# Applying the second layer's input-norm weight to the projection's weight pieces instead of to the transposed rows

## The reference

```python
def rms_norm(x, w):
    xf = x.astype(jnp.float32)
    xf = xf * lax.rsqrt(jnp.mean(xf * xf, axis=-1, keepdims=True) + RMS_EPS)
    return (xf * w.astype(jnp.float32)).astype(x.dtype)
...
    for layer in range(DEPTH):
        j = layer // 2
        h = rms_norm(x, norm_mix_w[layer])
...
            mix = retention_mixer(h, odd_w_in[j], ret_norm_w[j], odd_w_out[j])
        x = x + mix
        h = rms_norm(x, norm_ffn_w[layer])
        x = x + hierarchical_moe(h, router_c_w[layer], router_c_b[layer], router_f_w[layer], router_f_b[layer],
                                 moe_w_gate_up[layer], moe_w_down[layer])
...
def retention_mixer(h, w_in, norm_w, w_out):
    q, k, v, g = split_cols(h @ w_in, ODD_SPLITS)
```

## Time and profile before

| | us |
|---|---|
| median of 3 runs | 1178.06 (1177.57 to 1178.78) |
| profiled execution | 1180.1 |
| its span | 1178.3 |
| PE busy (share of the span) | 1111.0 (94%) |
| DVE busy | 699.3 (59%) |
| ACT busy | 608.7 (52%) |
| POOL busy | 395.7 (34%) |
| chain that ended last: PE / DVE / DMA / ACT | 83% / 7% / 3% / 3% |

### The profile page before, as it was taken

How to read it: one execution, slowest core, us unless ns; L and a number is a source line. 1 busy time by engine, 2 the same in 40 slices (tenths; PEclk the granted TensorE clock), 3 DMA queues, 4 the chain that set the end, 5 groups by cost and what they waited for, 6 DMA issues and landing times.

```text
span 1178.3 us, 19724 instructions
## 1 busy us (share of the span) xinstructions
PE 1111.0 (94%) x7062; PEld 912.4 (77%) x7063; DVE 699.3 (59%) x1016; ACT 608.7 (52%) x903; POOL 395.7 (34%) x344
## 2 busy tenths in 40 slices
PE   8999999999998899998999999999999997999990
PEld 5778887778787688886788888888888886788870
DVE  5435444368736999996646341543432138999975
ACT  5556234242434699995633342233342234899971
POOL 4343221110133244332155325442234442344332
PEclk8999999999999899999999999999999998999995
DMA  9333311112225699996443213331222364999945
GB/s 263 77 88 55 73 38 55 36 41 70 72 64 210 244 358 379 382 365 225 181 128 98 81 56 106 94 108 58 81 73 90 98 198 161 355 381 377 381 191 223
DMA packets 81668, 194.76 MB, mean 165 GB/s; under 512 B 20349, under 2 KB 21433, under 8 KB 80825
## 3 DMA queue, kind: packets, MB, share of 16 engines
q1 hardware_dynamic: 59368, 159.34, 40.2%
q10 hardware_dynamic: 12432, 17.60, 4.4%
q0 software_dynamic: 9792, 16.80, 3.8%
HBM read 189.50 MB, written 23.07 MB: 180 GB/s over the span
## 4 chain that ended last, share of the span: by engine, by line
PE 83%; DVE 7%; DMA 3%; ACT 3%; issue 1%; ACTq 1%; POOL 0%; POOLq 0%; DVEq 0%
PE ps L673 24%; PE ps L675 23%; PE ps L674 23%; PE ps L2572 2%; PE ps L2364 2%; DMA arena<-y 1%; DVE x L1469 1%; PE ps L2247 1%; ACTq L1423 1%; PE ps L2500 1%; DMA arena<-hs,slot_rows 1%; PE ps L2637 1%; PE ps L2201 1%; ACT wh L1006 1%; DMA y<-arena,cur_rows 1%
## 5 line engine op out<-in xcount | busy, mean ns | idle before, releaser
L840 POOL TENSOR_TENSOR wl<-raw,wh 128x1024 fp32r<-128x1024 f32 x94 | 228.6, 2440 | 380.4 <-ACT wh L1006 380.1
L673 PE MATMUL ps<-wh,hT_hi 128*128 128x512 f32 x864 | 347.3, 402 | 2.9 <-DVE hT_lo L1988 2.4
L675 PE MATMUL ps<-wh,hT_lo 128*128 128x512 f32 x864 | 338.4, 392 | 0.0
L674 PE MATMUL ps<-wl,hT_hi 128*128 128x512 f32 x864 | 337.9, 391 | 0.0
L1006 ACT ACTIVATE wh<-raw 128x1024 fp32r<-128x1024 f32 x116 | 122.4, 1068 | 213.0 <-PE ps L675 191.3
L673 PEld LDWEIGHTS ps<-wh,hT_hi 128*128 128x128 f32 x864 | 163.1, 189 | 38.1 <-DVE hT_lo L1988 2.9
L675 PEld LDWEIGHTS ps<-wh,hT_lo 128*128 128x128 f32 x864 | 162.6, 188 | 34.5
L674 PEld LDWEIGHTS ps<-wl,hT_hi 128*128 128x128 f32 x864 | 163.0, 189 | 30.7
L673 PE MATMUL ps<-hT_hi,wh 128*128 128x512 f32 (+1 forms) x296 | 117.0, 395 | 2.0 <-DVE arena_rounded L1820 1.0
L1963 DVE TENSOR_TENSOR wl<-arena,wh 128x1024 fp32r<-128x1024 f32 x96 | 113.6, 1222 | 5.6 <-ACT wh L1293 5.3
L674 PE MATMUL ps<-hT_lo,wh 128*128 128x512 f32 (+1 forms) x296 | 114.5, 387 | 0.0
(11 more groups left out here) (331 smaller groups left out, 1581.1 us busy)
## 6 DMA issues: line engine op xcount, KB each, us to landing
raw<-in_moe_w_gate_up_dram SPq DMA_DIRECT2D x64, 512.0 KB, 9.7
arena<-in_moe_w_gate_up_dram SPq DMA_DIRECT2D x64, 512.0 KB, 9.6
raw<-in_odd_w_in_dram SPq DMA_DIRECT2D x48, 512.0 KB, 3.8
raw<-in_even_w_in_dram SPq DMA_DIRECT2D x32, 512.0 KB, 4.8
arena<-in_moe_w_down_dram SPq DMA_DIRECT2D x32, 512.0 KB, 10.1
raw<-in_moe_w_down_dram SPq DMA_DIRECT2D x32, 512.0 KB, 12.8
raw<-in_odd_w_out_dram SPq DMA_DIRECT2D x16, 512.0 KB, 3.5
arena<-y ACTq DMA_DIRECT2D x6, 1024.0 KB, 9.8
```

The lines of the kernel that those rows point to most:

```text
L673: nc.tensor.matmul(dst, lh, rh, start=first, stop=False)
L674: nc.tensor.matmul(dst, lh, rl, start=False, stop=False)
L675: return nc.tensor.matmul(dst, ll, rh, start=False, stop=last)
L840: pool.tensor_tensor(columns_of(i, wl[:, i % NSPL, :, :]), raw_columns(i), columns_of(i, wh[:, i % NSPL, :, :]).bitcast(F32), ALU.subtract ...
```

## The change

The norm's weight `nw1` is no longer applied to the transposed rows. `transposed` and `lo_tiles` now do for n = 2 what they do for n = 0: two instructions of 128 x 512 on each engine for a tile. Instead the weight, which in a raw piece is one column for each of its two 128 x 512 halves, is applied to the 48 pieces of blocks 10 to 21. For the first four the high part is two activations with the scale (`hi`) and the low part two instructions on DVE that multiply and subtract. For the other 44 a new step `fold_norm` multiplies the raw piece in place on ACT, two activations of 128 x 512, one piece ahead of the piece's own `hi`; the four of block 11 are folded inside `norm(2)`, two ahead of `transposed` of tile 2 and two ahead of that of tile 3.

Orders change too. On ACT, `hi` of block 10's last piece moves behind the loads of the MoE outputs, and `square` of a tile comes directly after its `transposed`. On DVE the low part of tile 0 moves ahead of `combine` of tile 1, and that of tile 1 behind `combine` of tile 2, as before. On PE the first fillers go from 22 to 20, the second from 3 to 2 and now follow tile 0's transposes; the rows of a tile with pieces 0 to 2 come before the next tile's transposes and not after them. POOL's and SP's orders don't change. Line numbers shift: L1029, L1020, L1062, L1370, L1242, L2111, L2144 and L2169 of before are L1049, L1043, L1079, L1388, L1259, L2127, L2162 and L2184 of after; in after, L1021 is the plain `hi`, L1018 and L1019 the one with the scale, L1029 is `fold_norm`, L1774 and L1775 the folded low part, L682 to L684 the three products.

```diff
+        def norm_folded(i):
+            return first_piece(10) <= i < first_piece(22)
+        def folded_columns(i):
+            k = 2 * ((i - first_piece(10)) % 4)
+            return [nw1[:, k + k2:k + k2 + 1] for k2 in range(2)]
...
                 wait_spl_free(act, i)
+                if norm_folded(i) and lo_by_dve(i):
+                    act.wait_ge(s_("wb_loaded"), 32)
+                    w = folded_columns(i)
+                    A(act.activation(wh[:, i % NSPL, 0, :], raw_at(i)[:, 0, :], ACT.Copy, scale=w[0]))
+                    act.activation(wh[:, i % NSPL, 1, :], raw_at(i)[:, 1, :], ACT.Copy, scale=w[1]).then_inc(hi_done, 1)
+                    return
                 act.activation(columns_of(i, wh[:, i % NSPL, :, :]), raw_columns(i), ACT.Copy).then_inc(hi_done, 1)
+            def fold_norm(i):
+                if not norm_folded(i):
+                    return
+                act.wait_ge(raw_loaded[RAW_SLOTS[i]], 16 * raw_load(i))
+                for x, w in zip((raw_at(i)[:, 0, :], raw_at(i)[:, 1, :]), folded_columns(i)):
+                    A(act.activation(x, x, ACT.Copy, scale=w))
...
-                    if n == 2:
-                        for j in range(4):
-                            k = 4 * g + j
-                            A(act.activation(HTH[:, k, cols(T)], tile(name)[:, cols(j)], ACT.Copy, scale=nw1[:, k:k + 1]),
-                              s_("hT_hi_made") if j == 3 else None)
-                        continue
                     A(act.activation(HTH[:, 4 * g:4 * g + 4, cols(T)], v3(tile(name), 4), ACT.Copy), s_("hT_hi_made"))
...
-                    act.wait_ge(s_("wb_loaded"), 32)
-                    transposed(n, 0)
                     for T in range(NT):
-                        if T + 1 < NT:
-                            transposed(n, T + 1)
+                        if T > 1:
+                            for i in (2 * T, 2 * T + 1):
+                                fold_norm(first_piece(10) + i)
+                        transposed(n, T)
                         square(n, T)
                     roots()
...
-                for i in range(4):
+                for i in range(3):
                     hi(m + 6 * NE + i)
...
                     act.dma_start(YP[:, T, :, :], src[T]).then_inc(s_(f"yp_loaded{T}"), 16)
+                hi(m + 6 * NE + 3)
...
                     for i in splits_at(step):
                         hi(i)
+                    if k == "piece":
+                        fold_norm(first_piece(step[1]) + step[2] + 4)
...
-                    combine(0, 0, 0)
-                    combine(0, 0, 1)
-                    combine(0, 1, 0)
-                    combine(0, 1, 1)
-                    dve.wait_ge(s_("wb_loaded"), 32)
                     for T in range(NT):
-                        lo_tiles(("hT", n, T), T)
-                        if T + 2 < NT:
-                            combine(0, T + 2, 0)
-                            combine(0, T + 2, 1)
+                        combine(0, T, 0)
+                        combine(0, T, 1)
+                        if T > 1:
+                            lo_tiles(("hT", n, T - 1), T - 1)
+                        elif T == 0:
+                            lo_tiles(("hT", n, 0), 0)
+                    lo_tiles(("hT", n, NT - 1), NT - 1)
...
             def norm(n):
                 if n == 2:
-                    keep_busy(22)
+                    keep_busy(20)
                 for T in range(NT):
+                    if n == 2 and T > 0:
+                        rows(MOE_AT[0], T - 1, (0, 1, 2))
...
-                        if T == 1:
-                            keep_busy(3)
-                        if T > 1:
-                            rows(MOE_AT[0], T - 2, (3,))
-                        if 0 < T < NT - 1:
-                            rows(MOE_AT[0], T - 1, (0, 1, 2))
+                        if T == 0:
+                            keep_busy(2)
+                        else:
+                            rows(MOE_AT[0], T - 1, (3,))
...
                 if n == 2:
-                    rows(MOE_AT[0], 2)
-                    rows(MOE_AT[0], 3)
+                    rows(MOE_AT[0], NT - 1)
```

More of the change, by code:

```diff
@@ L1568, in lo_tiles @@
                     hi, lo = (x[:, 4 * g:4 * g + 4, cols(T)] for x in ((HTH2, HTL2) if name[0:3] == ("yT", 1, 0) else (HTH, HTL)))
-                    if name[0:2] == ("hT", 2):
-                        for j in range(4):
-                            k = 4 * g + j
-                            ins = stt(lo[:, j, :], tile(nm)[:, cols(j)], nw1[:, k:k + 1], hi[:, j, :].bitcast(F32), ALU.mult, ALU.subtract)
-                            if j < 3:
-                                D(ins)
-                            else:
-                                D.read(ins, nm)
-                    elif name[0:2] == ("yT", 0):
+                    if name[0:2] == ("yT", 0):
                         D.read(stt(lo, v3(tile(nm), 4), head_w[:, g:g + 1], hi.bitcast(F32), ALU.mult, ALU.subtract), nm)
@@ L1760, in lo @@
                 wait_spl_free(dve, i)
+                if norm_folded(i):
+                    w = folded_columns(i)
+                    hi, low, r = (x.bitcast(F32) if n == 0 else x for n, x in enumerate((wh[:, i % NSPL, :, :], wl[:, i % NSPL, :, :], raw_at(i))))
+                    D(stt(low[:, 0, :], r[:, 0, :], w[0], hi[:, 0, :], ALU.mult, ALU.subtract))
+                    stt(low[:, 1, :], r[:, 1, :], w[1], hi[:, 1, :], ALU.mult, ALU.subtract).then_inc(lo_dve, 1)
+                    return
                 tt(wl[:, i % NSPL, :, :], raw_at(i), wh[:, i % NSPL, :, :].bitcast(F32), ALU.subtract).then_inc(lo_dve, 1)
```

## The result

The changed kernel takes 1183.84 us (median of 20 runs, 1181.13 to 1188.0); the kernel before, run as often beside it, 1179.47 (1177.34 to 1187.04). The ratio is 1.0035, 95% interval 1.0022 to 1.0048: 4.1 us **slower**, 2.6 to 5.7. The forecast was +2.1 us, and its range ended at 1181.4. Some of the miss is the base: the three runs of before that were known then lay 1.4 us under the median of twenty. The other part is in the terms, and the trace shows which.

A forecast was written before the change was run, and what follows sets the result against it. PE, busy 94% of the span, was taken to bound the kernel. Restart +0.9, folds +0.1 and clock +1.1 make +2.1 us on the median 1178.06: 1180.2 us, range 1178.2 to 1181.4.

The forecast's parts named there:

- case A: The forecast itself, chance 0.50: ACT's end sets the restart and PE's clock falls; 1.5 to 2.9 us above the median.
- Part 1: Stage's head: block 10's last high part behind ACT's load issues delays DVE's low part and tile 0's addition; cost 0.3 us.
- part 2 or 3: Stage: tile 0's products 3.7 us sooner, tile 3's transposes 4.0 later; ACT's end 12.04 us, PE's restart +0.9 us.
- Part 4: Folds of 44 pieces on ACT, mostly hidden except at value-block evacuations: +0.1 us, bounds 0 and 4.4.
- Rival D: Chance 0.13: in-place fold pairs of 3 us, not 1.47, hold PSUM at value-block evacuations; 1182 to 1184 us.
- Part 5: PE's clock falls to the lower level after about 2.7 us idle ahead of block 11: +1.1 us.
- Rival B: Chance 0.28: same end on ACT, but PE's clock stays high; 1179.1 us, bounds 1178.4 and 1179.6.
- rival C: Chance 0.09: the gain arrives, ACT's work behind tile 3 overlaps more and PE's own end counts; 1176.3 us.

The follow-up runs named there:

- x_lo3: The changed kernel, but DVE adds tile 0's MoE outputs ahead of the low part of block 10's last piece; ratio to before 1.0012.
- x_twice: The changed kernel with each in-place fold followed by a second pass without a factor, so a fold takes 2.8 us; ratio to before 1.0072.
- x_fold: The changed kernel, but at value blocks 13, 18 and 19 the fold comes behind the block's evacuation, not ahead of it; ratio to before 1.0028.
- x_fill: The changed kernel with four more fillers on PE behind the roots, in a PSUM bank nobody uses; ratio to before 1.0025.
- x_evac: The changed kernel, but ACT makes only block 11's first high part, then evacuates block 10, then makes the other two; ratio to before 1.0018.
- x_hi3: The changed kernel with the high part of block 10's last piece back ahead of the MoE output loads on ACT; ratio to before 1.0046.
- x_best: The changed kernel with 18 fillers, x_lo3, x_half (pieces 0 and 1 ahead of the next transposes), x_evac and x_fold together; ratio to before 0.9958.
- x_hi3b: The changed kernel with the high part of block 10's last piece ahead of the MoE output loads and 18 fillers, not 20; ratio to before 1.0042.
- b_evac: The kernel before, but ACT makes only block 11's first high part, then evacuates block 10, then makes the other two; ratio to before 1.0009.
- x_rows: The changed kernel's orders on all engines, but with the weight at the transposed rows as in the kernel before, no fold; ratio to before 1.0141.
- x_half: The changed kernel, but only a tile's products with pieces 0 and 1, not 0 to 2, precede the next tile's transposes; ratio to before 1.0030.

## Why the prediction was too low

The mechanism in the stage is the one that was forecast as case A, and the trace follows it closely: a tile of 7.10 us (7.06 forecast), tile 3's transposes as the thing that comes late, the end of 12.04 us behind them (12.04), the restart released by DVE's low part, 2.54 us of idle time (2.7) and a fall of the clock. Three terms were too small.

*Part 1, the head: forecast +0.3 us, measured 1.5 at the additions (558.08 against 556.54).* The step took ACT's end of the issues from the trace of before, 553.63. In the change it is 554.98: the folded high parts reach the first issue 0.34 us later, and the three large loads take 2.76 us to issue, not 1.74. So DVE's low part ended 1.35 us later than worked out, and all that follows came later with it. Nothing else in part 2 or 3 is off by more than 0.2 us: 0.9 forecast for the restart and 1.35 from the head make the 2.3 measured. x_lo3 takes 1.9 us off by one step at this place, since its additions start sooner even than before's.

*Part 4, the folds: forecast +0.1, measured 0.9.* The place was right (a high part followed at once by a value block's evacuation) and two of the three places paid 0.45 us each, with a fold as long as forecast, 1.47 us. A value near the lower bound had no row behind it: the slack was not read. It stands in the trace of before, in the evacuation that the earlier trace rows break off after its second instruction. ACT by time, the kernel before, its third and fourth:

```profile
666.77 0.69 ACT L1242 ACTIVATE arena_rounded<-ps,small 128x512 fp32r<-128x512 f32 x1 [0.38 <-PE ps L675]
668.13 0.69 ACT L1242 ACTIVATE arena_rounded<-ps,small 128x512 fp32r<-128x512 f32 x1 [0.67 <-PE ps L675]
```

ACT waited for PE 0.38 + 0.67 = 1.05 us there. A fold of 1.47 us uses that up and is 0.42 too long, which is the step. Block 19 has the same two pauses in the kernel before and the same step; block 18 has 2.3 us of them and no step. x_twice agrees: 2.8 - 1.05 is 1.8, measured 1.8 to 1.9; and x_fold takes both steps away. Rival D had this mechanism, but asked for a fold of 2 us or more; the fold need not be longer than forecast.

*Part 5, the clock: forecast 1.1, measured 1.65.* The whole stretch lay on PE's work, the upper of the two bounds, and not half of it on idle time. (The forecast's own rows, 0.42 and 0.23 us, make 1.5 and not 1.6 of a stretch of 3.3 us.)

The range did not cover this: its bounds took at most 0.3 us more for the head, where 1.2 more were measured, and +0.1 for the folds throughout, though part 4 gave 4.4 as its upper bound. Case A's lower end was added up wrongly as well: 0.4, 0.1 and 0.7 make 1.2 and not 1.5.

Together: 2.3 + 0.9 + 1.65 = 4.85, the measured distance of 4.8. Rival B fails on the clock, rival C on tile 3's transposes. The sentence of the Trainium skill that PE's clock is gated when idle (Advanced Engine Details and Errata, Clock Domains) fits x_fill, where PE idled 0.40 us and the clock stayed at 1.00; that idling alone is not enough, x_evac (1.52 us) and x_hi3 (3.07 us, below) show once more. The Trainium skill's sentence against simple arithmetic on ScalarE (Trainium Architecture — The Big Picture, The five engines, in one table) is not borne out as a reason here: what the folds cost is set by their place in ACT's order, and x_fold removes the 0.9 us with the folds still on ACT.

Not settled: why the three loads took 2.4 to 2.9 us to issue in most of these kernels and 1.6 to 1.8 in others (before 1.74, x_best 1.60, x_hi3b 1.81, b_evac and x_rows 1.77). Where it is long, one of the three, the first or the second, takes 1.4 to 1.9 us, and the other two about 0.5 each.

## What to carry to other kernels

An edit that moves an engine's first product forward is worth nothing if it also puts more products ahead of the last tile's inputs: follow the last tile, and the engine that ends last behind it, and not the first. Work that is hidden "on average" on an engine two thirds idle still costs where it stands between the last input and a release: add up the pauses right behind it in the old trace (1.05 us here, against a fold of 1.47), or move it one step. The time that an engine takes to issue the same transfers is not a constant to be taken from the old trace: here it was 1.60 to 2.85 us for the same three loads.

## What the runs showed that was not expected

Length of idle time did not fully sort the falls of PE's clock. Ahead of block 11 it fell behind 1.92 us (x_half) and 2.53 us (x_lo3), and did not behind 3.07 us in x_hi3, the longest of all. PE by time, x_hi3, the roots and the first product of block 11:

```profile
587.85 1.05 PE L2183 MATMUL ps<-arena,small 128*128 128x128 f32 x8
591.98 0.47 PE L682 MATMUL ps<-hT_hi,wh 128*128 128x512 f32 x1 [3.07 <-DVE arena_rounded L1835]
```

The fillers of x_hi3, 46 us sooner, started behind 1.81 us of idle time and did run at the low clock; the other thirteen traces have 1.81 to 1.90 us there too, and no fall. Two stretches of x_hi3, under the fillers and behind the restart, columns as above:

```profile
545.90:549.20 3.30, 3.30 (x7) 2.03 (x7) 3.23 (x5) 3.20 (x6) 0.32 (x1) 0.50 0.22 84
592.00:595.00 3.00, 3.00 (x13) 2.49 (x14) 2.86 (x5) 2.90 (x5) 3.00 (x2) 1.00 0.64 184
```

So a pause of two to three microseconds was likely to cost some 1.65 us here (six of seven restarts of block 11), but it is not a fixed price; that this is why the runs of one kernel spread by several us is possible and not shown.
